# A two-block transformer kernel: the first norm applied to turned tokens by quarters of its width, its weight sums in PSUM, and the attention bias rows made four heads at a time

## The chip, the cores and the metric

The kernel runs on one core of a Trainium2 chip. The metric is the device time of one execution in microseconds (us). TensorE (PE) multiplies matrices into PSUM; VectorE (DVE) and ScalarE (ACT) read PSUM and SBUF; GpSimd (POOL) works on SBUF; SyncE (SP) issues most transfers and ACT a few.

## What is computed

A first block (retention and dilated attention in parallel, then an MLP) is followed by two layers of a second block (latent attention, mLSTM and SSD in parallel, then experts). All is float32. The change touches the entry of the first block and the attention's bias:

```python
def rms_norm(x, g):
    y = xf * lax.rsqrt(jnp.mean(xf * xf, axis=-1, keepdims=True) + RMS_EPS)
    return (y * g.astype(jnp.float32)).astype(x.dtype)
def modulate(h, shift, scale):
    return h * (1 + scale[:, None, :]) + shift[:, None, :]
mod = jax.nn.silu(c) @ w_ada[l] + b_ada[l]             # c (1,1024), w_ada (1024,6144)
sh1, sc1, g1, sh2, sc2, g2 = jnp.split(mod, 6, axis=-1)
h = modulate(rms_norm(x, norm1_g[l]), sh1, sc1)         # x (1,256,1024)
...
proj = h @ w_in                                         # w_in (1024, 12800)
...
bias = bias_tab[t5_bucket(jnp.clip(m, 0, w) * dilation)]   # 12 heads in 3 groups, 32 buckets
s = (jnp.einsum('bhrnid,bhrnjd->bhrnij', qs, kb) * (dh ** -0.5) + bias[None, :, None, None])
```

## The kernel before

**Weights.** Weights come as units of 128 x 1024 floats, two to a piece of 1 MB, by one in-order queue (SP) into the ring `w_raw` (8 slots; in the first 96 units, slots 0 to 5 hold weights and slots 6 and 7 pieces of `w_ada`). Each unit is split: ACT rounds it to `w_hi` (`hi`, L784), POOL subtracts to get `w_lo` (`lo`, L721, two instructions of 512 columns for a unit), for the few units in `DVE_LO` DVE does it (`dve_lo`, L2255), and PE multiplies three times (`mm3`, L1302 to L1304). `w_hi` and `w_lo` have four slots, so ACT can be four units ahead of PE. A unit of the retention's input is 12 matmuls of 512 columns.

**The start.** The first shift and scale are sums over 1024 inputs: DVE adds `w * silu(c)` over eight chunks of 128 rows (`ada_half`, L2265), and PE adds over the partitions by a matmul with ones (`half_sums`, L1526), which leaves the row on all partitions. It is done by two halves of 512 channels; in the second, PE takes three of the eight chunks itself (`half_chunk`, L1520). Then ACT copies the rows out of PSUM (`half_rows`, L873, L875), DVE forms the normed and modulated tokens (`first_normed`: L2311, L2245, L2318), PE transposes them (L1575), ACT rounds (`turned_half`, L881) and DVE subtracts (L2324). After each half, PE runs that half of the first three tiles (units 0 to 5, then 6 to 11; `PRE` = 3). The ready signs are semaphores: `t_lo` for the turned tokens, `unit_used` for a unit that PE is done with.

**Bias rows.** For each of 12 heads, PE multiplies a one-hot table by that head's column, broadcast to 128 columns (`bias_row_of`, L1503), ACT copies the 128 equal rows out (L863), and one transfer stores 3 MB to the scratch `rel_scratch` (L891; `bias_stored`), which is read back shifted by a row per partition (L936).

**What follows.** DVE goes on in the order `dve_lo(1)`, `ada_piece(0)`, `rotate(0)`, `ada_piece(1)`, `rotate(1)` and so on. SP issues, in its order, the piece of `w_ada` for `ada_piece(1)` only after `ada_piece(0)`, and behind it the piece with units 12 and 13:

```python
for s in range(2 if r == 1 else 0, n_ring):
    if s == n_ring - 1:
        sp.wait_ge(ada_used, ADA_FIRST + PIECE * r)
```

DVE waits for the bias store ahead of reading tile 6 out of PSUM, since tile 6 takes the place of the bias rows:

```python
ada_piece(4)
dve.wait_ge(bias_stored, 16)
ret_in_tile(6)
group_norm(0)
```

PE waits in turn before tile j of 8 and 9 until DVE has read tile j - 2 (`g_free`), and for units 43, 47 and 51 on DVE's `dve_lo(2)` to `dve_lo(4)`.

## Time and profile before

| | before |
|---|---|
| median of 3 runs | 1369.2 us (1365.95 to 1369.45) |
| profiled execution, its time | 1369.16 us |
| its span, first to last instruction | 1367.4 us |
| granted TensorE clock, mean | 0.994 of full |
| PE busy | 1309.5 us (96%) |
| DVE busy | 881.9 us (64%) |
| ACT busy | 736.4 us (54%) |
| POOL busy | 638.9 us (47%) |
| moved by DMA | 280.03 MB, 205 GB/s in the mean |

The span is 1.8 us shorter than the execution's time; instants below are us from the span's start. Busy shares say how long an engine had work; which wait ended last is read from the chain of waits and from each engine's order of time.

### The profile page before, as it was taken

How to read it: one execution, taken by the hardware profiler on the slowest of the kernel's cores; microseconds unless marked ns; L12 is line 12 of the kernel's file. 1: busy time of each engine (PE TensorE's matmuls, PEld its weight loads, DVE VectorE, ACT ScalarE, POOL GpSimd, SP SyncE). 2: the span in 40 equal slices, each digit the busy share in tenths (PEclk: the TensorE clock that was granted, in tenths of full speed). 3: DMA queues.
4: the chain of work that ended last, by engine and by line, in shares of the span. 5: the costliest groups of instructions: out<-in, count | busy, mean ns of one | idle time of the engine just before them, and what ended most of it. 6: DMA issues, size and time to landing. Idle time of an engine off the chain costs nothing.

```text
span 1367.4 us, 18658 instructions
## 1 busy us (share of the span) xinstructions
PE 1309.5 (96%) x6684; PEld 1085.4 (79%) x6684; DVE 881.9 (64%) x1383; ACT 736.4 (54%) x1107; POOL 638.9 (47%) x512
## 2 busy tenths in 40 slices
PE   7999999999998999999999999999989999899997
PEld 4778787899886788888787787888868877788885
DVE  6684873345343565223678667888868867788777
ACT  5343444444464544445566428666745663567664
POOL 3898888988858699999400420000051034000000
PEclk9999999999999999999999999999999999999999
DMA  9867468646444555555532008879755200588782
GB/s 375 312 262 305 157 243 292 242 182 245 187 154 142 167 185 188 197 191 183 203 127 81 1 21 315 313 289 336 281 186 182 94 31 1 222 316 293 283 312 97
DMA packets 45496, 280.03 MB, mean 205 GB/s; under 512 B 5565, under 2 KB 8893, under 8 KB 13918
## 3 DMA queue, kind: packets, MB, share of 16 engines
q1 hardware_dynamic: 38434, 263.82, 53.3%
q10 hardware_dynamic: 6974, 15.05, 3.1%
q8 instruction: 53, 0.87, 0.3%
q14 instruction: 35, 0.29, 0.1%
HBM read 274.66 MB, written 4.19 MB: 204 GB/s over the span
## 4 chain that ended last, share of the span: by engine, by line
PE 74%; DVE 11%; POOL 5%; DVEq 3%; ACT 3%; issue 2%; DMA 1%; ACTq 1%; SPq 0%; POOLq 0%
PE AC L1302 9%; PE AC L1304 9%; PE AC L1303 9%; PE G L1302 8%; PE G L1304 8%; PE G L1303 8%; POOL w_lo L721 5%; PE T L1492 2%; PE G L1492 2%; DVE w_lo L2172 2%; DMA w_raw<-w_stream 1%; PE G L1340 1%; PE G L1339 1%; PE G L1338 1%; PE T L1493 1%
## 5 line engine op out<-in xcount | busy, mean ns | idle before, releaser
L721 POOL TENSOR_TENSOR w_lo<-w_raw,w_hi 128x512 fp32r<-128x512 f32 (+1 forms) x470 | 610.5, 1334 | 332.5 <-ACT w_hi L784 321.0
L784 ACT ACTIVATE w_hi<-w_raw 128x1024 fp32r<-128x1024 f32 x444 | 467.0, 1058 | 392.1 <-PE AC L1304 172.4
L2172 DVE TENSOR_TENSOR w_lo<-w_raw,w_hi 128x1024 fp32r<-128x1024 f32 x228 | 275.7, 1224 | 52.6 <-ACT w_hi L784 44.7
L1302 PE MATMUL AC<-w_hi,yT_hi 128*128 128x512 f32 x368 | 145.3, 395 | 0.9 <-POOL w_lo L721 0.9
L1304 PE MATMUL AC<-w_hi,yT_lo 128*128 128x512 f32 x368 | 142.7, 388 | 0.0
L1303 PE MATMUL AC<-w_lo,yT_hi 128*128 128x512 f32 x368 | 142.5, 387 | 0.0
L1302 PE MATMUL G<-w_hi,arena_r 128*128 128x512 f32 x320 | 128.2, 401 | 4.3 <-DVE w_lo L3042 2.2
L1304 PE MATMUL G<-w_hi,arena_r 128*128 128x512 f32 x320 | 125.1, 391 | 0.0
L1303 PE MATMUL G<-w_lo,arena_r 128*128 128x512 f32 x320 | 124.7, 390 | 0.0
L1302 PE MATMUL G<-w_hi,xT 128*128 128x512 f32 (+1 forms) x240 | 98.5, 410 | 5.4 <-DVE xT L2324 2.1
L1302 PE MATMUL AC<-w_hi,xT 128*128 128x512 f32 x240 | 98.4, 410 | 3.4 <-POOL w_lo L721 3.4
L1304 PE MATMUL AC<-w_hi,xT 128*128 128x512 f32 x240 | 94.4, 393 | 0.0
L1303 PE MATMUL AC<-w_lo,xT 128*128 128x512 f32 x240 | 94.2, 392 | 0.0
L1304 PE MATMUL G<-w_hi,xT 128*128 128x512 f32 (+1 forms) x240 | 93.9, 391 | 0.0
L1303 PE MATMUL G<-w_lo,xT 128*128 128x512 f32 (+1 forms) x240 | 93.6, 390 | 0.0
L759 POOL TENSOR_TENSOR arena<-arena,scr 128x256 f32<-128x256 f32 (+1 forms) x16 | 9.0, 595 | 161.5 <-ACT arena L1183 161.5
L1302 PEld LDWEIGHTS AC<-w_hi,yT_hi 128*128 128x128 f32 x368 | 69.1, 188 | 16.6 <-POOL w_lo L721 2.1
L1304 PEld LDWEIGHTS AC<-w_hi,yT_lo 128*128 128x128 f32 x368 | 69.1, 188 | 14.5
L1303 PEld LDWEIGHTS AC<-w_lo,yT_hi 128*128 128x128 f32 x368 | 69.2, 188 | 13.6 <-issue 0.2
L1302 PEld LDWEIGHTS G<-w_hi,arena_r 128*128 128x128 f32 x320 | 60.1, 188 | 17.2 <-DVE arena_r L3036 2.6
L1304 PEld LDWEIGHTS G<-w_hi,arena_r 128*128 128x128 f32 x320 | 60.0, 188 | 13.1
L1303 PEld LDWEIGHTS G<-w_lo,arena_r 128*128 128x128 f32 x320 | 60.2, 188 | 11.5
(514 smaller groups left out, 2539.5 us busy)
## 6 DMA issues: line engine op xcount, KB each, us to landing
w_raw<-w_stream SPq DMA_DIRECT2D x148, 1024.0 KB, 5.0
w_raw<-w_expert SPq DMA_DIRECT2D x94, 1024.0 KB, 5.3
arena<-w_stream SPq DMA_DIRECT2D x8, 512.0 KB, 13.3
mod<-rows ACTq DMA_DIRECT2D x2, 2048.0 KB, 9.5
rel_scratch<-arena ACTq DMA_DIRECT2D x1, 3072.0 KB, 12.5
w_raw<-w_expert SPq DMA_DIRECT2D x4, 512.0 KB, 4.4
mod<-rows ACTq DMA_DIRECT2D x3, 476.0 KB, 4.1
x_sb<-x SPq DMA_DIRECT2D x1, 1024.0 KB, 8.8
```

Of the source, the lines that this page charges most:

```text
L721: i = pool.tensor_tensor(w_lo[:, k % SLOTS, cols], w_raw[:, raw, cols], w_hi[:, k % SLOTS, cols].bitcast(F32), ALU.subtract)
L759: i = pool.tensor_tensor(sw[:, j % 4, st, a:b], sw[:, j % 4, st, a:b], cbs[j // 4][:, st * S + a:st * S + b], ALU.mult)
L784: act.activation(w_hi[:, k % SLOTS, :], w_raw[:, raw, :], ACT.Copy).then_inc(hi_ready, 1)
L1302: pe.matmul(out, xh, wh, start=start, stop=False)
L1303: pe.matmul(out, xh, wl, start=False, stop=False)
L1304: return pe.matmul(out, xl, wh, start=False, stop=stop)
L1338: pe.matmul(out, w_hi[:, s, w], xT_hi[:, c, :], start=c == 0, stop=False)
L1339: pe.matmul(out, w_hi[:, s, w], xT_lo[:, c, :], start=False, stop=False)
L1340: i = pe.matmul(out, w_lo[:, s, w], xT_hi[:, c, :], start=False, stop=c == KC - 1)
L1492: pe.matmul(bank.rearrange("p (x n) -> p x n", x=2), w_hi[:, s, w], xT[:, c, :, :], start=c == 0, stop=False)
L1493: i = pe.matmul(bank[:, 0:S], w_lo[:, s, w], xT_hi[:, c, :], start=False, stop=c == KC - 1)
L2172: dve.tensor_tensor(w_lo[:, k % SLOTS, :], w_raw[:, k % RAW, :], w_hi[:, k % SLOTS, :].bitcast(F32), ALU.subtract).then_inc(lo_ready, 1)
```

## The change

The first norm's weights come by four quarters of 256 channels (shift and scale side by side, 512 columns), each as two pieces. DVE keeps the running sum in a PSUM bank. PE turns the tokens before they are modulated: ACT first multiplies them by 1/rms, PE transposes two chunks, and DVE applies scale and shift as numbers per partition, which it gets from four matmuls with one column. PE no longer takes chunks of the sum. It runs short matmuls in between (`keep_busy`). The bias rows of a group come from one pair of matmuls with 4 columns, stand on four partitions, and the store repeats each 128 times. `norm1_g` comes as a column instead of a row on all partitions. `DVE_LO` has unit 10 in the place of unit 8.

```diff
-DVE_LO = [U_RET_IN, U_RET_IN + 2 * SLOTS] + [U_RET_IN + UP * j - 1 for j in (11, 12, 13)]
+ADA_FIRST = QUARTERS * KC
+DVE_LO = [U_RET_IN, U_RET_IN + 10] + [U_RET_IN + UP * j - 1 for j in (11, 12, 13)]
...
+            first_units(0)
+            first_units(1)
+            quarter(1)
+            sp.wait_ge(ada_used, KC // 2)
+            piece(2 * n_ring + 2, 2)
+            quarter(2)
+            lows_done(PIECE)
+            piece(3 * n_ring, 0)
+            sp.wait_ge(ada_used, 2 * KC)
+            quarter(3)
+            lows_done(2 * PIECE)
+            piece(3 * n_ring + 1, 1)
...
+            act.wait_ge(rstd_done, 1)
+            for t in range(TOK):
+                act.activation(xs[:, t, :], x_sb[:, t, :], ACT.Copy, scale=var[t]).then_inc(h_ready, HALVES)
...
-            act.wait_ge(bias_rows_out, N_AH)
-            act.dma_start(A["rel_scratch"][:, 0:P, :].rearrange("h p n -> p h n"), bias_vec).then_inc(bias_stored, 16)
-            turned_half(1)
+            for q in range(1, QUARTERS):
+                turned_quarter(q)
+                his(U_RET_IN + PRE * q + 2, U_RET_IN + min(PRE * (q + 1) + 2, PRE * UP - 1))
+            act.wait_ge(bias_rows_out, len(GROUPS))
+            for g in range(len(GROUPS)):
+                act.dma_start(A["rel_scratch"][g * AH:(g + 1) * AH, 0:P, :],
+                              bias_vec[:, g, :].unsqueeze(1).to_broadcast([AH, P, NT])).then_inc(bias_stored, 16)
...
+            def quarter_turn(q):
+                for i in range(QC):
+                    for t in range(TOK):
+                        c = QC * q + i
+                        o = pe.transpose(turn_bank(q)[:, i * S + t * P:i * S + (t + 1) * P], xs[:, t, c * P:(c + 1) * P], ident[:, :])
+                o.then_inc(t_ready, 1)
+            def quarter_sums(q):
+                pe.wait_ge(ada_summed, q + 1)
+                for i in range(2 * QC):
+                    o = pe.matmul(sum_cols(q)[:, i:i + 1], mod1[:, q, i * P:(i + 1) * P], ones_col, start=True, stop=True)
+                o.then_inc(scale_sum, 1)
+            for g in range(len(GROUPS)):
+                bias_rows_of(g)
+            pe.wait_ge(ident_loaded, 32)
+            keep_busy(G[:, 0, :], 10)
+            pe.wait_ge(h_ready, HALVES * TOK)
+            quarter_turn(0)
+            keep_busy(G[:, 0, :], 2)
+            quarter_sums(0)
+            keep_busy(G[:, 0, :], 10)
...
+            for u in range(QUARTERS):
+                pe.wait_ge(t_lo, T_H1 + u + 1)
                 for j in range(PRE):
...
+                        if t == 0 and j == PRE - 1 and u + 1 < QUARTERS:
+                            quarter_sums(u + 1)
+                    i.then_inc(unit_used, 1)
+                    if j == 0 and u + 1 < QUARTERS:
+                        quarter_turn(u + 1)
...
+            def turned_quarter(q):
+                dve.wait_ge(scale_sum, q + 1)
+                dve.scalar_tensor_tensor(a_col[:, cols], sum_cols(q)[:, QC:2 * QC], 1.0, g_col[:, cols], ALU.add, ALU.mult)
+                dve.tensor_copy(s_col[:, cols], sum_cols(q)[:, 0:QC])
+                dep()
+                for i in range(QC):
+                    c = QC * q + i
+                    o = dve.tensor_scalar(h_full[:, i * S:(i + 1) * S], turn_bank(q)[:, i * S:(i + 1) * S],
+                                          a_col[:, c:c + 1], s_col[:, c:c + 1], ALU.mult, ALU.add)
...
-            dve.wait_ge(bias_stored, 16)
+            dve.wait_ge(bias_stored, 16 * len(GROUPS))
             ret_in_tile(6)
```

**How the instructions move, on ACT, around the store of the bias rows.** `rel_scratch` is the scratch in memory, `xT` the turned tokens, `w_hi` a rounded unit. Before:

```order
L784 ACTIVATE w_hi<-w_raw 128x1024 x7
L873 ACTIVATE mod<-T 128x512
L875 ACTIVATE mod<-T 128x512
L891 DMA rel_scratch<-arena 128x12x512
L881 ACTIVATE xT<-T 128x4x128 x2
```

In the change:

```order
L882 ACTIVATE xT<-arena 128x2x256
L793 ACTIVATE w_hi<-w_raw 128x1024 x3
L882 ACTIVATE xT<-arena 128x2x256
L896 DMA rel_scratch<-arena 4x128x512 x3
L793 ACTIVATE w_hi<-w_raw 128x1024 x5
```

The store stood ahead of the second half's rounding (two instructions on `xT`); now it stands behind the fourth quarter's, and it reads 4 partitions instead of 128.

**On DVE, between the last part of the norm and the first rotation.** `mod<-w_raw,sm,mod` x2 is `ada_piece(0)`. Before:

```order
L2265 SCALAR_TENSOR_TENSOR mod<-arena,sm,mod 128x1024 x5
L2267 MEMSET sm 128x1
L2311 SCALAR_TENSOR_TENSOR arena<-mod,arena 128x512
L2245 SCALAR_TENSOR_TENSOR arena<-x_sb,sm,arena 128x512 x2
L2318 TENSOR_TENSOR arena<-arena,mod 128x512 x2
L2324 TENSOR_TENSOR xT<-T,xT 128x4x128 x2
L2255 TENSOR_TENSOR w_lo<-w_raw,w_hi 128x1024
L2277 SCALAR_TENSOR_TENSOR mod<-w_raw,sm,mod 128x1024 x2
```

In the change:

```order
L2262 SCALAR_TENSOR_TENSOR T<-arena,sm,mod 128x512
L2262 SCALAR_TENSOR_TENSOR T<-arena,sm,T 128x512 x6
L2262 SCALAR_TENSOR_TENSOR mod<-arena,sm,T 128x512
L2266 MEMSET sm 128x1
L2312 SCALAR_TENSOR_TENSOR sm<-T,sm 128x2
L2313 COPY sm<-T 128x2
L2317 TENSOR_SCALAR arena<-T,sm 128x256 x2
L2322 TENSOR_TENSOR xT<-arena,xT 128x2x256
L2255 TENSOR_TENSOR w_lo<-w_raw,w_hi 128x1024
L2276 SCALAR_TENSOR_TENSOR mod<-w_raw,sm,mod 128x1024 x2
```

The first eight rows stand there once for each of the last three quarters (once more, in two parts, for the first); `ada_piece(0)` comes behind the fourth, as before it came behind the second half.

## Rows read from the trace of the kernel before

**Rows 1.** The page: busy time by engine, and the chain that ended last, by engine

```profile
PE 1309.5 (96%) x6684; PEld 1085.4 (79%) x6684; DVE 881.9 (64%) x1383; ACT 736.4 (54%) x1107; POOL 638.9 (47%) x512
PE 74%; DVE 11%; POOL 5%; DVEq 3%; ACT 3%; issue 2%; DMA 1%; ACTq 1%; SPq 0%; POOLq 0%
```

**Rows 2.** Timeline of PE, the start: start us, us, instruction, [idle before <-releaser]

```profile
26.47 1.17 PE L1575 MATMUL AC<-ident,arena 128*128 128x128 f32 x8 [1.27 <-DVE arena L2318]
28.81 0.53 PE L1302 MATMUL G<-w_hi,xT 128*128 128x512 f32 x1 [1.17 <-DVE xT L2324]
...
30.41 0.63 PE L1303 MATMUL G<-w_lo,xT 128*128 128x512 f32 x1
...
40.54 0.39 PE L1304 MATMUL AC<-w_hi,xT 128*128 128x512 f32 x1
40.76 0.39 PE L1302 MATMUL AC<-w_hi,xT 128*128 128x512 f32 x1
...
70.84 1.03 PE L1544 MATMUL T<-ident,arena 128*128 128x128 f32 x8
72.46 0.47 PE L1302 MATMUL AC<-w_hi,xT 128*128 128x512 f32 x1 [0.58 <-POOL w_lo L721]
```

**Rows 3.** The chain that ended last, in order of time, around unit 12

```profile
58.80 2.15 DVE mod L2277
60.97 0.33 SPq L596
61.29 0.05 issue
61.39 7.21 DMA w_raw<-w_stream
68.63 1.07 ACT w_hi L784
```

**Rows 4.** Timeline of DVE: the sums, a lone row of 512, and work beside POOL

```profile
23.37 0.69 DVE L2311 SCALAR_TENSOR_TENSOR arena<-mod,arena 128x512 f32<-128x512 f32 x1 [2.00 <-ACT mod L873]
...
56.40 4.54 DVE L2277 SCALAR_TENSOR_TENSOR mod<-w_raw,sm,mod 128x1024 f32<-128x1024 f32 x2
61.03 0.69 DVE L2343 TENSOR_TENSOR arena<-G,arena 128x512 f32<-128x512 f32 x1
...
63.60 1.54 DVE L2348 TENSOR_TENSOR arena<-arena 128x512 f32<-128x512 f32 x1
```

**Rows 5.** Timeline of ACT, the square sums and the store of the bias rows

```profile
17.34 1.05 ACT L866 ACTIVATE arena<-x_sb 128x1024 f32<-128x1024 f32 x1
...
49.49 0.41 ACTq L891 DMA_DIRECT2D rel_scratch<-arena  x1
```

**Rows 6.** DMA issues in 0 to 110 us: KB each, median us to landing

```profile
rel_scratch<-arena ACTq DMA_DIRECT2D x1, 3072.0 KB, 12.5
```

**Rows 7.** Busy time by stretch; the last three columns: PE clock, DMA share, GB/s

```profile
57.00:59.00 2.00, 2.00 (x10) 1.68 (x9) 1.91 (x2) 1.06 (x1) 2.00 (x2) 1.00 1.05 410
67.00:69.00 2.00, 2.00 (x10) 1.68 (x9) 1.91 (x2) 0.37 (x1) 0.00 (x0) 1.00 1.03 434
```

**Rows 8.** Timeline of DVE around the wait for the bias store, to `dve_lo(2)`

```profile
113.95 4.51 DVE L2277 SCALAR_TENSOR_TENSOR mod<-w_raw,sm,mod 128x1024 f32<-128x1024 f32 x2
124.44 1.22 DVE L2235 COPY arena<-G 128x1024 f32<-128x1024 f32 x1 [5.98 <-PE G L1304]
128.00 1.29 DVE L2366 BATCH_NORM_STATS2 sm<-arena 128x6 f32<-128x512 f32 x2 [2.34 <-ACT arena L918]
...
132.25 0.17 DVE L2198 RECIPROCAL sm<-sm 128x2 f32<-128x2 f32 x1 [2.15 <-ACT sm L812]
...
157.59 1.29 DVE L2366 BATCH_NORM_STATS2 sm<-arena 128x6 f32<-128x512 f32 x2 [1.37 <-ACT arena L918]
...
172.94 2.31 DVE L2255 TENSOR_TENSOR w_lo<-w_raw,w_hi 128x1024 fp32r<-128x1024 f32 x1
```

**Rows 9.** Timeline of PE: first matmul of tile 8, and of unit 43

```profile
142.76 0.48 PE L1302 MATMUL G<-w_hi,xT 128*128 128x512 f32 x1
...
178.00 0.39 PE L1302 MATMUL G<-w_hi,xT 128*128 128x512 f32 x1
```

**Rows 10.** Timeline of PE, eight matmuls of few columns and what follows them

```profile
833.18 0.96 PE L2102 MATMUL T<-sm,xT 128*128 128x16 f32 x8
833.99 0.49 PE L1302 MATMUL G<-w_hi,arena_r 128*128 128x512 f32 x1
```

More of the change, by code:

```diff
@@ L80 @@
 U_MIX = 16 * 6
-ADA_DVE = (range(0, KC), range(3, KC))
-ADA_PE = range(0, 3)
-ADA_FIRST = sum(len(r) for r in ADA_DVE)
-DVE_LO = [U_RET_IN, U_RET_IN + 2 * SLOTS] + [U_RET_IN + UP * j - 1 for j in (11, 12, 13)]
+QUARTERS = 4
+QC = KC // QUARTERS
+QW = 2 * QC * P
+ADA_FIRST = QUARTERS * KC
+N_SUMMED = QUARTERS - 2
+DVE_LO = [U_RET_IN, U_RET_IN + 10] + [U_RET_IN + UP * j - 1 for j in (11, 12, 13)]
 U_JOINED = U_ATT_FIRST + UP
@@ L211, in first_unit @@
 def first_unit(j, u):
[L213 removed]
+    return U_RET_IN + PRE * u + j
 def ret_tile_end(j):
@@ L271, in program @@
         AC_tok = AC[:, :, :].rearrange("p (t c) n -> p t (c n)", t=TOK)
-        half_landed = [sem("half_landed%d" % q) for q in range(KC // PIECE)]
+        quarter_landed = [sem("quarter_landed%d" % q) for q in range(2 * 2)]
         raw_landed = [sem("raw_landed%d" % s) for s in range(RAW // PIECE)]
@@ new lines, in _, with first_units, quarter @@
+            sp.dma_start(g_col, A["norm1_g"]).then_inc(ident_loaded, 16)
+            piece(0, 2)
+            sp.wait_ge(mod_cleared_a, 1)
+            sp.dma_start(mod[0:1, 0:2 * D], A["b_ada"][:, 0:2 * D]).then_inc(ada_b_loaded, 16)
+            piece(1, 3)
+            def first_units(s):
+                for u in range(PIECE):
+                    sp.dma_start(w_raw[:, s * PIECE + u, :], A["w_stream"][2 * n_ring + s][:, u * UNIT:(u + 1) * UNIT]).then_inc(raw_landed[s], 16)
+            def quarter(q):
+                for h in range(2):
+                    sp.dma_start(quarter_home[2 * q + h], A["w_stream"][2 * q + h]).then_inc(quarter_landed[2 * (q % 2) + h], 16)
@@ L860, in _ @@
             act.activation(csil, ccol, ACT.Silu).then_inc(c_ready, 1)
-            for h in range(N_AH):
-                act.wait_ge(bias_row, h + 1)
-                act.activation(bias_vec[:, h, :], row_banks[h % len(row_banks)], ACT.Copy).then_inc(bias_rows_out, 1)
             act.wait_ge(x_loaded, 16)
             for t in range(TOK):
-                i = act.activation(h_sb[:, t, :], x_sb[:, t, :], ACT.Square, accum_out=sm[:, 16 + t:17 + t])
+                i = act.activation(xs[:, t, :], x_sb[:, t, :], ACT.Square, accum_out=sm[:, 16 + t:17 + t])
@@ L867, in _ @@
             i.then_inc(sumsq_ready, 1)
             root(0, sm[:, 16:18])
-            def half_rows(c, shift, scale):
-                act.wait_ge(scale_sum, c + 1)
-                act.activation(mod1[:, c, 1, :], scale, ACT.Copy).then_inc(scale_out, 1)
-                act.wait_ge(mod_sum, c + 1)
-                act.activation(mod1[:, c, 0, :], shift, ACT.Copy).then_inc(mod_out, 1)
-            def turned_half(c):
-                for t in range(TOK):
-                    act.wait_ge(t_ready, T_H1 + HALVES * c + t + 1)
-                    act.activation(xT_hi[:, 4 * c:4 * c + 4, t * P:(t + 1) * P],
-                                   turn_bank(c, t).rearrange("p (c n) -> p c n", n=P), ACT.Copy).then_inc(t_hi, 1)
@@ L903, in _ @@
                 last = U_RET_IN + UP * (j + 2)
-                his(U_RET_IN + UP * (j + 1) + early, last - 1)
+                his(U_RET_IN + max(UP * (j + 1) + early, PRE * UP - 1), last - 1)
                 if len(copies) > TOK:
@@ L924, in _ @@
             act.wait_ge(y_ready, RH)
-            act.wait_ge(bias_stored, 16)
+            act.wait_ge(bias_stored, 16 * len(GROUPS))
             def load_bias(q):
@@ L1514, in mod_sums @@
                 k.then_inc(mod_sum, 1)
[L1516 to L1534 removed]
+            def quarter_turn(q):
[9 more added lines that the diff above has]
+                o.then_inc(scale_sum, 1)
+            for g in range(len(GROUPS)):
+                bias_rows_of(g)
[6 more added lines that the diff above has]
+            keep_busy(G[:, 0, :], 10)
             def ret_turn(j):
@@ L2330, in _ @@
+            dve_lo(0)
+            turned_quarter(0)
+            for q in range(1, QUARTERS):
+                for h in range(2):
+                    ada_quarter(q, h)
+                turned_quarter(q)
             dve_lo(1)
```

199 lines of the change are left out of this document (69 added, 130 removed).

## The prediction, made before the change was run

> **What bounds the kernel now.** I read the page first: PE is busy for 96% of the span and holds 74% of the chain that ended last [rows 1]. So outside a few places a change is worth what it takes from PE's idle and low-clock time or from waits of PE. Then the order of time on PE. The first weight matmul starts at 28.81, which waited for DVE's turned tokens; the twelve units of the first three tiles end at 70.84 and unit 12 starts at 72.46, which waited for POOL [rows 2]. A matmul of 512 columns takes 0.227 us there (40.54 to 40.76 and the like), at the first level 0.43 (2.4 and 1.2 GHz) [rows 2]. The chain shows what unit 12 really waited for: not PE, but DVE's `ada_piece(0)` (done at 60.95), behind it SP's issue, two pieces of 1 MB (61.3 to 68.6) and ACT's rounding [rows 3]. So the reader should see two clocks in the start: PE's own work up to 70.8, and DVE's, which gates unit 12 through SP. The third place is later: DVE stands ready at 118.5 (113.95 + 4.51) at the wait for the bias store, and reads tile 6 at 124.44, when PE has made it [rows 8]. The store was issued at 49.49 [rows 5] and took 12.5 us [rows 6], so that wait cost nothing; its slack is 118.5 - 62 = 56 us.
>
> **The early part, step by step.** Tokens are now issued second on SP and land near 6.5 (an estimate: 1 MB at 410 GB/s [rows 7] behind an issue at 1.6). The square sums are 2.2 us on ACT (two of 1.05 [rows 5], each with its read of the sum), root and reciprocal about 1 us behind DVE's first four sum steps; then ACT scales two token blocks (2.1 us), to 15.7. DVE's sum is 8 steps of 512 columns instead of 1024 for each quarter: 0.69 each (the row at 23.37 [rows 4]), about 0.8 with the drain, 6.4 us for a quarter, 25.6 in all. Whether PSUM sums help beside POOL: a row with a PSUM input took 0.69 while POOL worked, one with only SBUF took 1.54 [rows 4], and the old sums in that stretch 2.2 for 1024. So PSUM pays for six of eight steps. First quarter: pieces land near 9.4 and 12, DVE's eight steps end at 16.7, PE's sums near 18, scale and shift on DVE, ACT's rounding and DVE's subtraction (0.4 + 0.85 + 0.7 + 0.7) give the first turned quarter at 21.5. That is 7.3 us ahead of 28.81.
>
> A quarter on PE then costs: four transposes 0.6 (half of 1.17 [rows 2]), the first 2.5 units 6.8 (30 x 0.227), the sums 0.83 (8 records in 0.81 [rows 10]), and then the path sums, 0.4 + 0.85 on DVE, 0.7 on ACT, up to 1.5 on DVE (two SBUF inputs beside POOL [rows 4]), with 0.3 of signals: 11.9 to 12.2, of which PE idles about 2. DVE's next sums (6.4 to 7.4) just fit under the 7.4 before PE asks. Three such quarters put the fourth turned quarter at 21.5 + 3 x 12.2 = 58.1. The clock: PE ran at the low level from 28.81 for nine matmuls (0.43 instead of 0.227) after a stretch with little work [rows 2], 1.8 us; I take 1.5 for the same here, so 59.6. Removed are `half_chunk` (3.4 us of PE), 12 head rows on PE and ACT, which lay under the start anyway, and the 0.5 MB of `norm1_g`.
>
> PE is done with the twelve units at 59.6 + 3 x 2.7 = 67.8, 3 us sooner than 70.84. But DVE: `dve_lo(1)` 1.35 and `ada_piece(0)` 4.54 [rows 4] end at 65.5, against 60.95. SP's two pieces, ACT and POOL follow as before (11.5 us [rows 2, 3]), so unit 12 starts at 77.0, **4.6 us later**. From there the order is the old one. By itself the early part gives 1369.2 + 4.6 = 1373.8. POOL is not moved past anything but its two waits, which go.
>
> **The store.** Three transfers of 1 MB are issued behind the fourth quarter's rounding, near 60 instead of 49.5. Each reads four partitions 128 times. No row shows such a transfer. Bounds from rows: at the rate of all 16 engines, 410 to 434 GB/s [rows 7], 3.15 MB take 7.5 us. At the share of the rate that one partition has in a transfer over all 128 (434 / 128 = 3.4 GB/s), four partitions send 3.15 MB in 231 us. Between them is one sixteenth of the whole, 27.1 GB/s, that is 116 us: the part of the rate that eight of 128 partitions have. I take this one, because four neighbouring partitions are less than that group and I see no reason for them to get more than the path of their group; it is also the middle of the two ends on a scale of ratios. The Trainium skill says so outright (SBUF — State Buffer, Door 1: The DMA port swizzle): partitions 0 to 3 lie behind one of 16 ports, 27 GB/s; by it the store would take 116 us, and no run here shows it.
>
> So `bias_stored` comes at 60 + 116 = 176, not at 62. DVE stands at its wait from 118.5 (a few us later by the above) to 176. Queued behind it on DVE: tile 6's read, three group norms, `ada_piece(5)` and `(6)`, `dve_lo(2)`. PE meets it first at tile 8, which it began at 142.76 [rows 9] and which now begins at 177.2 (34 us late), and again at unit 43, whose low part is DVE's. From tile 6's read to the end of `dve_lo(2)` DVE took 124.44 to 175.25, 50.8 us, of which 5.9 were waits for ACT's copies (2.34 + 2.15 + 1.37 [rows 8]) that will have been made. So unit 43 starts at 176 + 44.9 = 220.9, against 178.00 [rows 9]: **42.9 us later**. The 4.6 us of the early part are under this wait, and so is what weights lose to the store (the group norms' rows wait behind it on ACT's ring, too, to about 180, inside DVE's 44.9). Nothing behind unit 43 gives it back: PE's waits there are few.
>
> The profiled execution took 1369.16, the median is 1369.2, so both give the same sum: 1369.2 + 42.9 = **1412**. Each us of the store is a us of the kernel once it ends after 133. The store's own range, 111 to 125 us with a start of 57 to 63, gives 1404 to 1424.
>
> **Rivals.** (1) **The store is held only by its engines.** If the transfer is cut by its first dimension of four, four of 16 engines carry it, 4 x 25.6 GB/s [rows 7]: 30.7 us, done at 91, far before 118.5. Then no stall; but units 12 and 13's pieces share these four engines, 5 us become 10, and unit 12 comes 4.6 + 5 later: 1379 (1372 to 1386). For it: a transfer of before never needed more of a partition than its share, so nothing rules it out. The Trainium skill (DMA: Bandwidth & Descriptors, Why a DMA increments its semaphore by 16) has the cut into as many engines as the slowest dimension allows, here four; taken alone it gives this time.
> (2) **Faster: the start is shorter than I sum.** The mechanism is DVE's arrival at `ada_piece(0)`, the price is 1 us for each us, and it decides if the fourth turned quarter is there before 55.0 (59.6 - 4.6). With 20.5 for the first, quarters of 11.2 and no low clock it would be there at 54.1, and `ada_piece(0)` would take 3 instead of 4.5 where POOL is idle: 2.4 to 5 us sooner, 1364 to 1367. For it: PSUM sums at 0.69 and POOL's empty stretch while PE waits. Against it: it needs the store to be harmless as well.
> (3) **Worse.** The store interleaves with the weight pieces on its engines and gets half of their time, or gets only its partitions' share, and ends at 230 to 290; or ACT's queue is held by three long stores so that no unit is rounded. 1369 + 97 and more: 1440 to 1520.
> (4) That the change does not do what it says: its PSUM sums could cost what SBUF sums cost (2.2 for 1024), 28 us of DVE instead of 25.6. That lies inside (1) and the stall.
>
> **The numbers.** Stall by one sixteenth of the rate, 1412: 0.55. Rival 1: 0.17 (0.13 of it slower than 1373.3, 0.04 within 0.3%). Rival 2: 0.18 (0.14 faster than 1365.1, 0.04 within). Rival 3: 0.10. Hence faster 0.14, within 0.3% 0.08, slower 0.78; 0.3% is 4 us, about what a measurement of this kernel can tell. The range reaches down to rival 2, 1362, and up to 1430, the stall's upper end with some loss of rate; rival 3 is left out, and 0.05 of the first. The likeliest case's own range is 1400 to 1430.
>
> **What the profile after would show.** The rows of DMA issues: `rel_scratch<-arena` x3 with 1 MB each and over 100 us to landing. DVE's read of tile 6 with some 55 us of idle before it, put down to a DMA or to nothing, near 176. PE idle for over 30 us before tile 8 and again before unit 43, its clock at the low level behind it. The first weight matmul at 20 to 23; the fourth quarter's at 57 to 62; unit 12 at 74 to 80. I am wrong if DVE reads tile 6 without having waited for the store; then the first matmul of unit 12 against 72.46 tells rivals 1 and 2 apart. If the store lands after 200, it is rival 3.

## The result, and where the time went

| | before | changed |
|---|---|---|
| median | 1368.6 us (1365.95 to 1369.45, 6 runs) | 1433.2 us (1432.0 to 1437.6, 6 runs) |
| ratio | 1 | 1.048, interval 1.047 to 1.049 |
| PE busy, profiled execution | 1309.5 us, 96% [rows 1] | 1305.8 us, 91% |
| span of the profiled execution | 1367.4 us | 1430.2 us |

The changed kernel is **4.8% slower**: 64.6 us, where 42.9 were forecast. PE has as much work as before (1305.8 against 1309.5 us), so all of the loss is idle PE. The page of the changed kernel, its busy times and its chain by engine:

```profile
PE 1305.8 (91%) x6718; PEld 1087.4 (76%) x6718; DVE 875.4 (61%) x1411; ACT 729.1 (51%) x1096; POOL 630.6 (44%) x512
...
PE 65%; DVE 12%; POOL 5%; DMA 5%; ACTq 5%; DVEq 3%; ACT 3%; issue 2%; SPq 0%; POOLq 0%
```

Against [rows 1], the chain lost nine points of PE and gained four of DMA and four of "ACTq", ACT's issuing of transfers. The timeline of PE (start, duration, instruction, idle before it) says when:

```profile
34.88 0.50 PE L1307 MATMUL G<-w_hi,xT 128*128 128x512 f32 x1 [1.27 <-DVE xT L2322]
...
57.19 0.50 PE L1307 MATMUL G<-w_hi,xT 128*128 128x512 f32 x1 [1.27 <-DVE xT L2322]
...
116.85 0.80 PE L1307 MATMUL AC<-w_hi,xT 128*128 128x512 f32 x1 [53.91 <-POOL w_lo L734]
...
122.06 1.04 PE L1552 MATMUL T<-ident,arena 128*128 128x128 f32 x8
122.86 0.47 PE L1307 MATMUL AC<-w_hi,xT 128*128 128x512 f32 x1
...
201.54 0.48 PE L1307 MATMUL G<-w_hi,xT 128*128 128x512 f32 x1
...
238.18 0.50 PE L1307 MATMUL G<-w_hi,xT 128*128 128x512 f32 x1 [0.29 <-DVE w_lo L2255]
```

57.19 is the fourth turned quarter. 116.85 is unit 11, the last of the first twelve, whose rounding stands behind the stores in ACT's order; its 12 matmuls run at the low clock (5.2 us instead of 2.7) and end at the transposes of 122.06, where the twelve ended at 70.84 before. 122.86 is unit 12, which was at 72.46 [rows 2]; 201.54 is tile 8, which was at 142.76, and 238.18 is unit 43, which was at 178.00 [rows 9]. So PE is 50.4 us late at unit 12, 58.8 at tile 8, 60.2 at unit 43, and 62.8 at the end of the profiled execution. The releaser that the row at 116.85 names, POOL, is only the last link. The timeline of ACT shows the first:

```profile
55.79 57.27 ACTq L896 DMA_DIRECT2D rel_scratch<-arena  x3
113.16 3.90 ACT L793 ACTIVATE w_hi<-w_raw 128x1024 fp32r<-128x1024 f32 x4 [56.75 <-issue]
```

and the view of that line alone (durations in ns, min/median/max):

```profile
L896 ACTq DMA_DIRECT2D rel_scratch<-arena x3: 278/17739/39188, 55.8 to 73.9; - x3
```

**To issue the three stores held ACT for 57 us** (0.3, 17.7 and 39.2), where the one store of before took 0.41 [rows 5]. Until they were out, ACT rounded no unit, so POOL had nothing to subtract and PE nothing to multiply. The windows view has what the transfer engines did while nothing else ran, and in the stretch behind it (the last three columns are PE's clock, the share of the 16 engines' time, GB/s):

```profile
92.00:112.00 20.00, 0.00 (x0) 0.00 (x0) 0.00 (x0) 0.00 (x0) 0.00 (x0) 0.50 0.23 25
114.00:186.00 72.00, 62.42 (x263) 49.93 (x264) 20.94 (x22) 22.17 (x27) 50.31 (x37) 0.90 0.70 228
```

The store alone moves 25 to 26 GB/s, against the 27.1 that the prediction took, and it keeps 0.23 of the engines' time busy doing so. DVE's side of it, in the timeline of DVE:

```profile
184.70 3.51 DVE L2276 SCALAR_TENSOR_TENSOR mod<-w_raw,sm,mod 128x1024 f32<-128x1024 f32 x2 [12.29 <-DMA w_raw<-w_stream]
188.75 1.23 DVE L2235 COPY arena<-G 128x1024 f32<-128x1024 f32 x1 [0.54 <-DMA rel_scratch<-arena]
...
198.53 2.03 DVE L2379 TENSOR_TENSOR arena<-arena,mod 128x1024 f32<-128x1024 f32 x1 [0.19 <-DMA arena<-gn_b]
...
235.81 2.31 DVE L2255 TENSOR_TENSOR w_lo<-w_raw,w_hi 128x1024 fp32r<-128x1024 f32 x1
```

These answer to [rows 8]. The store ended at 188, 132 us after its first issue. But DVE reached the wait for it only 0.54 us before its read, because PE and the weights were by then as late as the store (its `ada_piece` at 184.70 had itself waited 12.29 us for a landing). Right behind it DVE waited once more, 0.19 us before 198.53, for a row of the group norm, `gn_b`, and it is this that the chain that ended last goes through:

```profile
169.67 0.37 ACTq L916
170.08 28.36 DMA arena<-gn_b
```

`gn_b` stands behind the store in ACT's queue; before the change it landed 12.4 us after its issue. So there are three delays of nearly the same end, in parallel. From this trace alone it can't be told what the wait that was forecast would have cost by itself. That is what the first experiments are for.

The early part was not 4.6 us late: the turned quarters follow each other by 11.15 us (34.88, 46.02, 57.19), and `ada_piece(0)`, which gates unit 12's weights, ended at 60.84, against 60.95 [rows 3].

### The profile page after: what moved, and what is told of

Same layout as the page of the kernel before. It is cut to its first block, busy times and chain, and to the rows that moved or that the text cites. A ratio compares the mean times of both kernels' runs of the same rounds, so it can differ in the third digit from the quotient of the medians.

```text
span 1430.2 us, 18758 instructions
## 1 busy us (share of the span) xinstructions
PE 1305.8 (91%) x6718; PEld 1087.4 (76%) x6718; DVE 875.4 (61%) x1411; ACT 729.1 (51%) x1096; POOL 630.6 (44%) x512
## 4 chain that ended last, share of the span: by engine, by line
PE 65%; DVE 12%; POOL 5%; DMA 5%; ACTq 5%; DVEq 3%; ACT 3%; issue 2%; SPq 0%; POOLq 0%
PE AC L1307 8%; PE AC L1309 8%; PE AC L1308 8%; PE G L1307 7%; PE G L1309 7%; PE G L1308 7%; POOL w_lo L734 5%; ACTq L896 4%; DMA w_raw<-w_stream 2%; DMA arena<-gn_b 2%; PE T L1497 2%; PE G L1497 2%; DVE w_lo L2172 2%; PE G L1345 1%; PE G L1344 1%
## 5 line engine op out<-in xcount | busy, mean ns | idle before, releaser
L734 POOL TENSOR_TENSOR w_lo<-w_raw,w_hi 128x512 fp32r<-128x512 f32 (+1 forms) x470 | 603.2, 1319 | 403.6 <-ACT w_hi L793 396.2
L1307 PEld LDWEIGHTS AC<-w_hi,xT 128*128 128x128 f32 x240 | 46.0, 192 | 70.8 <-POOL w_lo L734 60.1
L2276 DVE SCALAR_TENSOR_TENSOR mod<-w_raw,sm,mod 128x1024 f32<-128x1024 f32 x32 | 58.0, 1814 | 48.5 <-DMA w_raw<-w_stream 46.9
L1307 PEld LDWEIGHTS AC<-w_hi,yT_hi 128*128 128x128 f32 x368 | 69.1, 188 | 16.7 <-POOL w_lo L734 2.2
L1307 PEld LDWEIGHTS G<-w_hi,arena_r 128*128 128x128 f32 x320 | 60.1, 188 | 17.5 <-DVE w_lo L2172 3.5
```

The costliest lines, as they stand in the source:

```text
L734: i = pool.tensor_tensor(w_lo[:, k % SLOTS, cols], w_raw[:, raw, cols], w_hi[:, k % SLOTS, cols].bitcast(F32), ALU.subtract)
L1307: pe.matmul(out, xh, wh, start=start, stop=False)
L2276: dve.scalar_tensor_tensor(m, w_raw[:, raw, :], csil[:, s:s + 1], m, ALU.mult, ALU.add).then_inc(ada_used, 1)
```

## Experiments: what in the store costs the time

Edits are to the changed kernel unless another is named. All times are medians; the kernel before stood at 1368.3 to 1369.2 beside them.

**1 (e1). The same bytes from 128 partitions.** The rows of the bias table are spread so that each head's row is computed on 32 partitions; the matmuls have as many columns as before.

```
-  row_banks = [AC[0:AH, 1 + g, :] ...]      bias_vec = arena[0:AH, 6144:7680]
+  row_banks = [AC[:, 1 + g, :] ...]         bias_vec = arena[:, 6144:7680]
-  act.dma_start(A["rel_scratch"][g * AH:(g + 1) * AH, 0:P, :], bias_vec[:, g, :].unsqueeze(1).to_broadcast([AH, P, NT]))
+  act.dma_start(A["rel_scratch"][g * AH * P:(g + 1) * AH * P, :].rearrange("(p i) n -> p i n", i=AH),
+                bias_vec[:, g, :].unsqueeze(1).to_broadcast([P, AH, NT]))
   (the scratch has no spare row per head any more; it is read back row for row as before)
```

> The changed kernel, with only the store's source altered: the bias rows are computed on 128 partitions (each head 32 times) instead of 4, three matmuls of the same 512 columns as before, and the same 3 MB are written by three transfers whose source has 128 partitions. Theory (all of the loss hangs on the store's four source partitions): the store lands within 15 us of its issue, as the 12.5 us of the kernel before; ACT's issues of it are short; tile 8 and unit 43 start where they started before the change (142.8 and 178.0, within 3 us). With the early part even (ada_piece(0) ended at 60.84 in the changed kernel, 60.95 before) the time is 1366 to 1372. Rival (the early part, or the sums in PSUM, cost something behind unit 12 by themselves): over 1376.

Measured: 1375.55 us, ratio 1.0044 (1.0029 to 1.0058), between the two ranges that were expected. So 57.6 of the 64.6 us hang on the source's four partitions. The three transfers landed 4.6, 8.6 and 14.7 us after their issues, and the view of its line shows the issues short again:

```profile
L896 ACTq DMA_DIRECT2D rel_scratch<-arena x3: 584/642/1411, 57.7 to 59.0; - x3
```

6.4 us over the kernel before stayed, more than expected; the second group of experiments is about them.

**2 (e3). As many partitions, but not neighbours.** Each row stands on four partitions, and the transfers read partitions 0, 4, 8 and 12.

```
-  bias_vec[:, g, :].unsqueeze(1).to_broadcast([AH, P, NT])
+  bias_vec[0:4 * AH:4, g, :].unsqueeze(1).to_broadcast([AH, P, NT])
```

> The changed kernel with each bias row held on four neighbouring partitions, and the three transfers read partitions 0, 4, 8 and 12 instead of 0, 1, 2 and 3: as many source partitions, descriptors and bytes as in the changed kernel, but no longer neighbours. Theory A (four neighbouring partitions share one path of one sixteenth of the rate): the store goes up to four times as fast, ends 30 to 45 us after its issue, ACT is held for about 15 us instead of 57, and the time is 1372 to 1390. Theory B (the rate is set by a transfer of only four rows, by four engines or by the source partition itself, wherever it stands): the store still takes about 130 us and the time is 1430 to 1437.

Measured: 1386.65 us, inside the range of Theory A. Two windows, the first with 0.29 MB of weights and 0.13 MB of the store, the second with the store alone (DMA view, same windows); the one above at 92 to 112, the store alone too, is to be held against the second:

```profile
72.00:76.00 4.00, 0.00 (x0) 0.00 (x0) 3.81 (x7) 0.00 (x0) 0.00 (x0) 0.50 0.25 104
76.00:78.00 2.00, 0.00 (x0) 0.00 (x0) 0.32 (x1) 0.00 (x0) 0.00 (x0) 0.50 0.26 101
```

Four times the rate (101 against 25 GB/s) for nearly the same share of the engines (0.26 and 0.23, about four of 16). So four neighbouring partitions share a path of 25 to 26 GB/s, and four partitions that are not neighbours don't. What stops the transfer next, at 101 or four times 25, can be four such paths or four engines. The first window speaks for the engines: two thirds of its bytes are weights, which don't come from those partitions, and the sum is 104 GB/s at a share of 0.25 all the same. The Trainium skill (SBUF — State Buffer, Door 1: The DMA port swizzle) puts partitions 0 to 3 on one port and 4, 8 and 12 on others; the trace agrees. It also says (DMA: Bandwidth & Descriptors, Why a DMA increments its semaphore by 16) that a transfer is cut into as many engines as its slowest dimension allows, four here; the share of 0.26 agrees. ACT was held for less, too (timeline of ACT), though for longer than the 15 us that Theory A had:

```profile
55.96 22.69 ACTq L896 DMA_DIRECT2D rel_scratch<-arena  x3
78.76 3.90 ACT L793 ACTIVATE w_hi<-w_raw 128x1024 fp32r<-128x1024 f32 x4 [22.17 <-issue]
```

The transfers themselves took 63 us in all, not 30 to 45: from 61 to 76 and again from 82 on, pieces of weights moved beside them.

**3 (e2). ACT not held in one piece.** The second and third store in pieces of 128 KB, one behind each rounding from unit 15 on.

```
+  store_rows(0, 0, P); rest = [(g, r, 16) for g in (1, 2) for r in range(0, P, 16)]
   hi(n, k)
+  if n == 0 and k >= 15 and rest: store_rows(*rest.pop(0))
```

> The changed kernel with the store of groups 1 and 2 cut into sixteen transfers of 128 KB, one issued behind each of ACT's roundings from unit 15 on; group 0 stays one transfer ahead of them. So ACT is not held for 57 us in one stretch. Theory T1 (what costs is the store's end, on which DVE waits with its arena): the store's end moves by less than 10 us, the time is 1420 to 1440. Theory T2 (what costs is ACT's queue, held by the long issues, so that no unit is rounded from 56 to 113): units 12 to 20 are rounded as they were before the change, and the time is 1375 to 1390. Theory T3 (what costs is the weight pieces, slowed on the engines or paths that the store fills): as T1, but with the pieces' landings of 20 us and more as in the changed kernel.

(The two waits for the store count its 17 transfers.) Measured: 1437.19 us, no gain. PE's timeline shows its stop in two instead of one:

```profile
89.02 0.76 PE L1314 MATMUL AC<-w_hi,xT 128*128 128x512 f32 x1 [20.83 <-POOL w_lo L734]
...
122.22 1.94 PE L1559 MATMUL T<-ident,arena 128*128 128x128 f32 x8 [7.45 <-ACT arena L912]
...
198.67 0.79 PE L1314 MATMUL G<-w_hi,xT 128*128 128x512 f32 x1 [21.13 <-DVE arena L2242]
```

Unit 12 came at 89.02 instead of 122.86, and then tile 8 waited 21.1 us for DVE's read of tile 6. That read is the forecast wait, seen at last, in the timeline of DVE:

```profile
197.39 1.22 DVE L2242 COPY arena<-G 128x1024 f32<-128x1024 f32 x1 [41.76 <-DMA rel_scratch<-arena]
```

The chain shows unit 12's piece of weights and the end of the store:

```profile
63.53 21.25 DMA w_raw<-w_stream
...
98.72 18.42 DMA w_raw<-w_stream
...
163.02 34.35 DMA rel_scratch<-arena
```

The store ended at 197.4, 9 us later than in one piece. The weight pieces of 1 MB took 21.3 and 18.4 us beside it, where unit 12's took 7.2 before [rows 3]: T3's sign is there as well as T1's.

**4 (e4). DVE doesn't wait for the store's end.** The rows are copied away first.

```
+  act.wait_ge(ada_used, 3 * KC)
+  act.activation(bias_home, bias_vec, ACT.Copy).then_inc(bias_rows_out, 1)
   (the stores read bias_home)
+  if j == 9: act.wait_ge(bias_stored, 16 * len(GROUPS))      (ACT, at its tenth retention load)
-  dve.wait_ge(bias_stored, 16 * len(GROUPS))
+  dve.wait_ge(bias_rows_out, len(GROUPS) + 1)
```

> The changed kernel with the source of the store moved to another place of the arena (one copy of 1536 columns on ACT, about 1.5 us), so that DVE needs not wait for the store's end ahead of tile 6; only ACT waits for it, at its tenth retention load. The ACT queue's long issues stay. Theory T1 (the store's end through DVE's wait is the cost): about 1390 to 1400. Theory T2 or T3 (ACT's held queue, or slowed weight pieces, are late by as much, so that the wait was only last by a little: 0.54 us of idle stood before DVE's first row behind it): 1425 to 1437.

Measured: 1435.14 us, no gain either, as T2 or T3 say. Its chain has ACT's issues in it, and behind them a transfer that stands behind the store in ACT's queue:

```profile
59.18 19.49 ACTq L899
78.70 37.59 ACTq L899
...
172.14 28.39 DMA arena<-gn_b
```

**5 (e5). Both edits at once.**

```
+  the lines of experiment 3 and those of experiment 4
```

> Both edits of e2_pieces and e4_no_wait at once, so that neither ACT's 57 us of issue nor DVE's wait for the store's end is left; what is left is that the store and the weight pieces use the same transfer engines. If the two holds cover for each other (each alone moved the time by nothing: 1437.2 and 1435.1), this kernel drops to 1380 to 1400. If the weight pieces themselves are slowed for as long as the store goes on (in e2_pieces the first piece took 21.25 us instead of 7.2, the next 18.4 and 18.2), it stays at 1425 to 1440.

Measured: 1418.54 us, outside both expectations. So the two holds do cover for each other, but what these edits take of them together is worth only 15 us. `gn_b` landed 32 us after its issue, behind the store's pieces, and DVE waited for it:

```profile
186.14 2.17 DVE L2391 TENSOR_TENSOR arena<-arena,mod 128x1024 f32<-128x1024 f32 x1 [8.60 <-DMA arena<-gn_b]
```

**6 (e11). And the group norms' rows on SP's queue.**

```
-  act.dma_start(mod[:, 0:2048], A["gn_g"] ...); act.dma_start(W, A["gn_b"] ...)      (at ACT's fifth retention load)
+  sp.wait_ge(t_lo, T_H1 + QUARTERS)
+  sp.dma_start(mod[:, 0:2048], A["gn_g"] ...); sp.dma_start(W, A["gn_b"] ...)        (behind the decay table)
```

> e5_pieces_no_wait, and the group norms' two rows of 1 MB go to SP's queue, behind the decay table, instead of ACT's, where they stood behind the store (gn_b was issued at 154.1 there and landed 32 us later, at 186, and DVE's first group norm waited for it). The store itself stays as slow. Theory A (the store's last hold on DVE is its place ahead of gn_b in ACT's queue): DVE's first group norm starts before 150, and the time falls from 1418.5 to 1385 to 1400. Theory B (the weight pieces, 16 to 21 us each beside the store instead of 7 to 13, are what is left): 1410 to 1420.

Measured: 1409.7 us. Theory B: 8.8 us were the place in the queue, and 40.5 us over the kernel before are left, with nothing on DVE waiting for the store. Two rows of the waits view of PE, 20 to 300 us (total, times, longest), hold nearly all of them:

```profile
PE AC L1318 <- POOL w_lo L737: 30.3, 7, 21.0
PE G L1318 <- POOL w_lo L737: 8.8, 4, 3.8
```

39.1 us of waits for low parts, hence for rounding. What the rounding waited for has two sides, though. The same view has them for ACT, and the timeline of ACT shows the second at work:

```profile
ACT w_hi L796 <- DMA w_raw<-w_stream: 51.9, 7, 24.3
ACT w_hi L796 <- issue: 20.2, 5, 4.3
```

```profile
144.53 1.06 ACT L796 ACTIVATE w_hi<-w_raw 128x1024 fp32r<-128x1024 f32 x1 [3.98 <-issue]
144.55 5.00 ACTq L801 DMA_DIRECT2D rel_scratch<-arena  x1
149.66 1.06 ACT L796 ACTIVATE w_hi<-w_raw 128x1024 fp32r<-128x1024 f32 x1 [4.06 <-issue]
149.67 5.22 ACTq L801 DMA_DIRECT2D rel_scratch<-arena  x1
154.99 1.06 ACT L796 ACTIVATE w_hi<-w_raw 128x1024 fp32r<-128x1024 f32 x1 [4.27 <-issue]
```

The pieces of the store, 128 KB each, still held ACT: one unit is rounded every 5.1 us there, where PE needs 2.7 for a unit. Set against the kernel before by ACT's own rows, unit 22 was rounded 21.3 us late (116.0 against 94.7) and unit 31 40.6 us late (165.0 against 124.4). So of the 40.5 us about 21 came up to unit 22, behind weight pieces that took 21.4 and 16.7 us to land, and about 19 came in the nine units behind it, whose roundings stand behind issues of pieces. ACT's hold was broken up in experiments 3, 5 and 6, not taken away, and none of them gives what it costs by itself.

Why weight pieces land late beside the store can be seen in the trace of the changed kernel. Its first three pieces, issued at 60.9, 61.3 and 65.1, landed at 78.9, 82.3 and 85.8; the windows view has this for the end of that stretch:

```profile
78.00:90.00 12.00, 0.00 (x0) 0.00 (x0) 6.34 (x8) 0.00 (x0) 0.00 (x0) 0.50 0.25 70
```

0.56 MB of the weights and 0.28 MB of the store moved there, and by the share of 0.25 it took the time of four of the 16 engines; the other twelve stood idle. So what was late of the pieces was the part on the engines that carry the store. No run moved the store to other engines than the weights use, so what this costs by itself was not measured.

**7 (e6). That part of the change alone**, put into the kernel before (rows for four heads at once, three stores; its first norm stays).

```
-  for h in range(N_AH): bias_row_of(h)
+  for g in range(len(GROUPS)): bias_rows_of(g)
-  act.dma_start(A["rel_scratch"][:, 0:P, :].rearrange("h p n -> p h n"), bias_vec)
+  for g in range(len(GROUPS)): act.dma_start(A["rel_scratch"][g * AH:(g + 1) * AH, 0:P, :], bias_vec[:, g, :] ... to_broadcast([AH, P, NT]))
```

> The kernel before, with only the part of the change that makes the bias rows for four heads at once and stores them from four partitions by three repeated transfers; its first norm stays as it was. Theory (the loss is the store's alone): issued at 49.5 instead of 56, the store ends near 182, and the time is 1369 + 55 to 66 = 1424 to 1435. Rival (the early part of the change carries a loss of its own, of the 6.4 us that e1_wide_store is above the kernel before): the time is 1424 or less, and the two parts add up to 1433.

Measured: 1445.04 us, above the expected 1424 to 1435, 76.6 over the kernel before and 12 over the whole change. There the store is issued ahead of the second half's rounding, so ACT's hold stops PE even sooner:

```profile
49.97 55.28 ACTq L892 DMA_DIRECT2D rel_scratch<-arena  x3
105.30 1.09 ACT L881 ACTIVATE xT<-T 128x512 fp32r<-128x512 f32 x2 [54.73 <-issue]
```

So the loss belongs to the store, and with the changed first norm it is 12 us smaller. The traces show where PE stands when the hold ends. In the changed kernel eleven of the first twelve units had been multiplied (PE stopped at 62.9) and unit 12's weights had landed. In e6 PE still had half of the twelve units before it, and `ada_piece(0)` and unit 12's piece (21.35 us) came only behind the hold; unit 12 started at 139.07, against 122.86.

## Experiments: what the new first norm is worth by itself

In experiment 1 (its profiled execution took 1377.6 us, 2.1 over its median), DVE's `ada_piece(0)` ended at 62.7 (1.8 us later than before the change, after a first quarter at the low clock: granted 0.50 and 0.67 in 20 to 24 and 24 to 28), and the wide store stood in front of two pieces of weights. The chain in order of time has 10.85 us for unit 12's piece instead of 7.21 [rows 3], and PE's timeline has unit 12:

```profile
63.18 10.85 DMA w_raw<-w_stream
```

```profile
77.83 0.77 PE L1306 MATMUL AC<-w_hi,xT 128*128 128x512 f32 x1 [8.75 <-POOL w_lo L734]
```

Unit 12 at 77.83 is 5.4 us later than in [rows 2]. Three kernels take these causes away one after the other.

**8 (e9). The wide store behind unit 15's rounding.**

```
   hi(n, k)
+  if k == 15 and late and late.pop(): store_rows()
```

> e1_wide_store with its three wide transfers issued behind ACT's rounding of unit 15 (near 75 us) instead of at 57.7, where they lie in front of the two pieces that units 12 and 13 wait for. Theory A (the 6.4 us that e1_wide_store lost are the store's collision with these pieces, the rest of 1.9 us a low clock in its first quarter): unit 12's rounding starts at 68 to 70 instead of 74.06, the time is 1368 to 1371. Theory B (the new first norm costs this elsewhere): 1375 as e1_wide_store.

**9 (e10). Units 12 and 13's piece ahead of the piece that waits for DVE**, on top of 8.

```
+  if r == 1 and s == n_ring - 1:
+      lows_done(RAW - PIECE + PIECE); piece(4 * n_ring, 0)
   if s == n_ring - 1:
       sp.wait_ge(ada_used, ADA_FIRST + PIECE * r)
```

> e9_wide_late, and on SP the piece with units 12 and 13 is issued ahead of the piece that waits for DVE's ada_piece(0). In the kernel before PE's own end of the first twelve units (70.8) hid what this could give; with turned quarters PE is done at about 68. Expected: unit 12 starts 4 to 6 us sooner than in e9_wide_late, and the time is 1362 to 1366, faster than both kernels. Rival (POOL's low parts, 18.8 us in one stretch behind the first rounding, are the bound behind unit 12 and start no sooner): no gain, within 1.5 us of e9_wide_late.

**10 (e17). More filler on PE ahead of the first turned quarter**, on top of 9.

```
-  keep_busy(G[:, 0, :], 10)
+  keep_busy(G[:, 0, :], 18)
   pe.wait_ge(h_ready, HALVES * TOK)
```

> e10_wide_late_swap with 36 instead of 20 filler matmuls ahead of the first turned quarter, as in e13_order_busy, which came out 2.4 us below e12_wide_late_order. Expected from that: 1369 to 1371, the same as the kernel before within what can be measured. Rival: in e10 the first quarter is not what sets unit 12 (DVE's rotations are), no change from 1372.2.

Measured: 1373.73, 1372.19 and **1370.96 us**. Each median is 1.2 to 1.8 us below the one before it. The intervals of neighbours overlap (ratios 1.0024 to 1.0048, 1.0020 to 1.0039 and 1.0009 to 1.0026), so only the way from e1 (1.0029 to 1.0058) to e17 is clear of noise, not each step. The last is 0.18% over the kernel before, less than the 0.3% that the prediction took as the bound of no change. e17 is where it was expected; e9 lies between its two ranges. None is faster, against the expectation of e10: unit 12 started at 75.18 in e9 and at 75.16 in e10, not 4 to 6 us sooner. The waits view of PE in the last, 20 to 300 us:

```profile
PE G L1316 <- DVE xT L2333: 3.8, 3, 1.3
PE AC L1316 <- DVE arena L2358: 3.4, 1, 3.4
PE T L1561 <- DVE arena L2361: 3.0, 1, 3.0
```

The weights of unit 12 are there, but PE waits for DVE's rotations of tiles 0 and 1, and unit 12 starts at 72.82, where it was. Before the change PE's own work ended there; now DVE's does. The fillers go with 1.2 us here and 2.4 in the pair below, both inside overlapping intervals. In the profiled executions the granted clock in 20 to 24 and 24 to 28 went from 0.50 and 0.78 (e10) to 0.69 and 1.00 (e17); but in e12, which has no more fillers than e10, it was 1.00 in both. So that the fillers gain by the clock is not shown.

**11. Another order on DVE and SP** could use the free time: e12 on top of 8, e13 with the fillers, e14 the same in the kernel before.

```
-  ada_piece(0); rotate(0); ada_piece(1); rotate(1); rotate(2); ada_piece(2); rotate(3); ada_piece(3)
+  rotate(0); rotate(1); ada_piece(0); rotate(2); rotate(3); ada_piece(1); ada_piece(2); ada_piece(3)
   (SP, by rounds r of three weight pieces and one ada piece)
-  weights(1), ada(1), weights(2), ada(2), weights(3), ada(3), ...
+  weights(1), weights(2), ada(1), ada(2), weights(3), ada(3), ...
```

> e9_wide_late with another order behind the start. In e10_wide_late_swap unit 12's weights were there, but PE waited 3.0 us for DVE's rotate(0) and 3.6 us for the first rows of rotate(1), both of which stand behind ada_piece(0) and ada_piece(1) on DVE. Here DVE rotates tiles 0 and 1 first, then ada_piece(0), tiles 2 and 3, then ada_piece(1); and SP issues the three pieces with units 12 to 17 ahead of the piece that waits for ada_piece(0), and so on by rounds. Theory A (DVE's order is what holds PE there): PE starts unit 12 near 70 instead of 75.2, and the time is 1365 to 1368. Rival (what is won here comes back as a wait for an ada piece or for POOL's low parts later): 1370 to 1374.

> e12_wide_late_order with 36 instead of 20 of PE's filler matmuls of 128 columns ahead of the first turned quarter, so that PE does not stand idle for about 3.6 us before it. In e1 and e10 the clock was at its lower level for the first quarter's weight matmuls (granted 0.50 and 0.67 in 20 to 24 and 24 to 28), which cost about 1.5 us. Expected: full clock from 22 on and 1 to 2 us less than e12_wide_late_order, 1363 to 1367. Rival: the filler holds the first turned quarter back, no change or 1 us more.

> The kernel before with the same new order on DVE and SP as in e12_wide_late_order. There PE's own work ended at 70.84 and unit 12 started at 72.46, so no more than 1.6 us is to be had: 1367 to 1369, no difference that three to five rounds show. If it gains as much as e12_wide_late_order did over e9_wide_late, the order and not the new first norm is what pays.

**12. The same with each round's weights ahead** (e15 on top of e13, and e16 in the kernel before).

```
-  weights(1), weights(2), ada(1), ada(2), weights(3), ada(3), ...
+  weights(1), weights(2), ada(1), weights(3), ada(2), weights(4), ada(3), ...
```

> e13_order_busy with one more step of SP's order: there the piece with units 18 and 19 still stood behind the piece that waits for DVE's ada_piece(1), and PE waited 14.9 us for POOL's low part of it. Here the weights of each round are issued ahead of the ada piece of the round before. Theory A (this wait was the only thing that took back what the order gave): PE's waits between 60 and 120 fall to under 3 us, against 6.6 in e10_wide_late_swap, and the time is 1363 to 1367, faster than the kernel before. Theory B (the piece's wait moves on to the next ada piece or DVE falls behind at its tile reads): 1370 to 1378.

> The kernel before with the same order on DVE and SP. Its PE has 1.6 us of wait at unit 12 and almost none behind it. Theory A: 1367 to 1369.5, no difference. If it comes out below 1366, the order pays by itself and the new first norm adds only the rest.

Measured: 1382.82 (e12), 1380.42 (e13), 1380.71 (e14), 1405.85 (e15), 1408.3 (e16), all five slower than was expected. In e12 PE waited 15.0 us for one low part, since the piece with units 18 and 19 stood behind a waiting piece. In e15 that wait was gone, and DVE starved in its place (waits view of DVE, 50 to 400 us; the kernel before has 4.0 us in that row):

```profile
DVE mod L2287 <- DMA w_raw<-w_stream: 96.5, 10, 17.4
```

The reading is that each `ada_piece` that comes later frees its slot later, and the next one lands later, so that the chain of ada pieces has no slack to lend. In the kernel before the same orders cost as much (11.5 us for e14 and 40.1 for e16; 9.1 for e12 over e9, 34.9 for e15 over e17), so they say little of the new start by themselves.

**13 (e18). A single rotation moved**, on top of 10.

```
-  ada_piece(0); rotate(0); ada_piece(1); rotate(1)
+  rotate(0); ada_piece(0); rotate(1); ada_piece(1)
+  lows_done(RAW - PIECE + PIECE * 2); piece(4 * n_ring + 1, 1)      (SP: units 14 and 15 ahead, too)
```

> e17_swap_busy, with only one rotation moved ahead on DVE (rotate(0), ada_piece(0), rotate(1), ada_piece(1)) and the pieces with units 12 to 15 ahead of the piece that waits for ada_piece(0). e12 to e16 moved more and starved DVE of ada pieces (96.5 us of waits in e15). Theory A (the new first norm can pay if DVE's order suits its start): PE no longer waits 3.0 us for rotate(0), unit 12 starts 1 to 3 us sooner, the time is 1366 to 1369. Theory B (each us that DVE's ada pieces are late returns in the ring): 1372 or more; then the order of the kernel before is near the best for either start, and the new first norm has nothing to win.

Measured: 1373.11 us, 2.2 over e17: PE's wait for rotate(0) went and unit 12 started at 70.62, 2.2 us sooner than in e17 (after 5.9 us of wait for rotate(1)). It was given back near 93, where PE waited 2.5 us for a low part and ran at the low clock behind it (granted 0.50 in 94 to 96), some 2 us more. In e12 unit 12 even started at 68.87. Theory B, as far as these orders tell: no version here beats the kernel before. Whether a better order exists stays open.

## Why the prediction was wrong

- **The step that failed** is the sentence "DVE stands at its wait from 118.5 ... to 176", with "PE meets it first at tile 8". DVE stood there for 0.54 us, and PE had met its delay before unit 12. The issue of a store was priced at its 0.41 us [rows 5] without a word; the three took 57. The sentence for it stands in rival 3, "ACT's queue is held by three long stores so that no unit is rounded", with 0.10 and a price of 1440 and more, for which no sum is given (the one sum there, 1369 + 97, is for a store that ends at 230 and comes to 1466, not 1440). What it did: unit 12 came 50.4 us late, of which 33.8 went when the hold was broken up (122.86 to 89.02, experiment 3), and with slow pieces behind it tile 8 was 58.8 late.
- **The rate of the store** was right: "27.1 GB/s, that is 116 us" against 25 to 26 alone in the trace. It began at 56, not 60, and took 132 us rather than 116: 1.40 of the 3.15 MB moved up to 113, the other 1.75 took 75 us, 23 GB/s, beside the weights. So DVE read tile 6 at 188.75, not at 176: **12.8 us of the 17.3 by which unit 43 was misjudged** (238.18 against 220.9).
- **DVE's way from tile 6 to `dve_lo(2)`**: 44.9 forecast, 49.4 measured (188.75 to 238.1), the other 4.5 us. The copies of ACT were not all made before, as was assumed: 1.09 and 0.98 of wait remain, with three shorter ones 2.8 in all. Where the rest comes from stays open.
- **Behind unit 43** nothing was to change; the profiled execution loses 2.6 us more there (60.2 to 62.8).
- **That the number was near** (1412 against 1433, a range up to 1430) is in part luck. With the store's real end, 188, the prediction's own sum gives 1424, by a wait that DVE hardly had. It comes out near because several delays of one store lie side by side and end near to where the store does. Experiments 3 to 6 show it: with ACT's hold broken up, or without DVE's wait, nothing moves; with both 15 us go; with the group norm's rows out of the queue 9 more; and 40.5 are left, about half behind late weights and half behind ACT's issues of the pieces. "The 4.6 us of the early part are under this wait, and so is what weights lose to the store" was the wrong way round: DVE's wait lay under ACT's hold and the late weights.
- **Rival 1** ("four of 16 engines carry it, 30.7 us", 1379) is not what the changed kernel does, but it is near what the kernel with partitions 0, 4, 8 and 12 does: 101 GB/s alone and 1386.65, just above its 1372 to 1386. There, too, ACT's hold of 22 us is what the rival had left out.
- **The early part**: +4.6 forecast, -0.1 measured at `ada_piece(0)`. The first turned quarter was put at 21.5 (its own terms, 18 + 2.65, give 20.65) and at 23 with the low clock; its matmuls start at 23.74. The quarter was put at 12.2 us and takes 11.15; the fourth turned quarter is there at 57.19 instead of 59.6, and `ada_piece(0)` takes 2.65 instead of 4.54, since POOL is idle then. Rival 2 named this way, with a price of 2.4 to 5 us sooner, if the fourth quarter is there before 55.0. It was not, and the gain didn't come with the store made harmless either: e17 is at 1371, and what PE waits for ahead of unit 12 there is DVE's rotations.

## What to carry to other kernels

Before a store is cut down to fewer source partitions to save compute, ask what the transfer does per path and per engine: the same 3 MB had landed 16 us after the first issue when they came from 128 partitions, and moved at 101 GB/s from four partitions in four groups and at 25 GB/s from four neighbours. A slow transfer also costs where nobody waits for its end: in the engine that issues it and in every transfer behind it in that queue; and in what others have on the engines that carry it. When removing one hold moves nothing, remove two before you call it harmless, and look in the trace if the hold has really gone: here a store in pieces held its engine piece by piece.

## What had not been expected of the hardware

- **Issuing a transfer can hold the engine until much of what was issued before has moved.** The first 1 MB store was issued in 0.28 us, the second in 17.7, the third in 39.2; ACT did nothing else in that time. The hold does not last until the transfers are through: when the third issue ended, ACT's queue had moved 1.40 of the 3.15 MB (DMA view, 50 to 113.06). With four times the rate the same issues took 0.7, 3.8 and 18.1 us, and 1.32 MB had moved at the end (experiment 2, 50 to 78.65); in experiment 7 it was 1.41 MB. From 128 partitions they took 0.6 to 1.4 us (experiment 1). Pieces of 128 KB took 4 to 7 us each to issue in experiment 6 from 112 us on.
- **A slow store goes with later landings of the others than its bytes would explain.** At 25 GB/s it kept 0.23 of the engines' time, and the weight pieces of 1 MB between 62 and 200 us took a median of 17.0 us, where the kernel before has 5.6 in that stretch. From 78 to 90 in the changed kernel the rest of three such pieces and the store moved on some four engines, at 70 GB/s in all, and the other twelve stood idle.
